# Three row buffers instead of four, and value tiles multiplied by column quarters, in the expert stage of a decoder step

## The chip, the cores and the metric

The kernel runs on one core of a Trainium2 chip. The metric is the time on the device in microseconds, the median of several runs.

## The reference

One layer of a decoder is applied to 256 prompt tokens and 8 x 8 sample tokens (320 rows of 2048): an attention with compressed, selected and window keys beside a short convolution, then an expert stage, then a gated embedding. The change lies in the expert stage. Each token picks, for each of 8 heads, 16 of 16384 experts; an expert is one row of `u_tab` and one row of `v_tab`, 2048 numbers each:

```python
def peer_ffn(n, wq, sub_keys, u_tab, v_tab):        # n: (320, 2048), normed
    ...
        g = jax.nn.softmax(fv, axis=-1)             # fv, eidx: the 16 best of each head
        act = jax.nn.gelu(jnp.einsum("td,trkd->trk", xc, u_tab[eidx]).astype(jnp.float32))
        return jnp.einsum("trk,trkd->td", (g * act).astype(xc.dtype), v_tab[eidx])
```

So every token reads 128 rows of `u_tab` (key rows) and 128 of `v_tab` (value rows), 8 KB each: 671 MB in all. The result is added to the residual `h`.

## The kernel before

Five engines run programs of their own and meet at semaphores. After the projections and the first attention work (about 750 us), the expert stage begins and goes on to about 2590 us. It is cut into 10 tiles `i` of 32 tokens, and each tile into 8 steps (`SSTEP`), 80 steps `k` in all (`STEPS`). On the 128 partitions of a step's tile lie 32 tokens four times over, and a step handles four rows `j` for each partition: four key tiles and four value tiles of 128 x 2048 floats.

A step passes through the engines like this:
- POOL (L586 to L601) issues four gathers of key rows into `u_row[0..3]` (L595), then four of value rows into `v_row[0..3]` (L600). Before it reuses a buffer it waits on `u_used` for key rows and on `v_used` for value rows. It works strictly in this order, and at a tile's first step it first waits for the indices (`idx_ready`).
- DVE (`group`, L1324) multiplies each key tile with the tokens' rows `n_rep` and sums along the row (L1333, one pass a tile, which gives `u_used`), waits for the GELU of ACT (`gelu`, L882), weighs the four results and builds `diag`, four 128x32 matrices that carry the weights (L1342, once a step).
- PE (`weighted_rows`, L1810) multiplies the value tiles with `diag` (L1821), in pairs `j = 0, 1` and `j = 2, 3`. Tile `j` writes column group `j` (partitions 32j to 32j+31) of four banks, one for each quarter `q` of the 2048 columns, so four partial sums of a quarter lie above each other. `v_used` goes up by 2 after each pair.
- At a tile's end ACT copies the banks to `acc` (`acc_out`, L886), PE adds the four groups with `sel` (L1830, 4 matmuls, `red_mm`), and DVE adds the result to `h` (`add_peer`, L1353, `h_seen`). PE starts the next tile's values only after `h_seen`. `acc_out` works in the same `acc` of which the first 32 partitions serve to stage the token rows of tiles 1 to 3 (`stage_rows`, L848, `spread_staged`).

Other work stands between the steps: in steps 0 to 31 (`EARLY`) PE runs `item(k)` (L1776) ahead of `weighted_rows(k)`, that is the rest of the attention, the projection with `w_out` (L1752, L1756) and the queries with `peer_wq` (L1772), with weights that SP loads. On DVE, pieces of `pick` (L1268) choose the next tile's experts between the steps. In steps 64 to 79 PE runs the gate matmuls (L1876) of the prompt after `weighted_rows(k)`. After step 79 come the gate of the sample rows and the outputs.

## Time and profile before

| what | value |
|---|---|
| median of 3 runs | 2659.68 us (2645.7 to 2661.2) |
| the profiled execution | 2654.51 us, of which the span of the page is 2652.7 us |
| granted TensorE clock, mean of the span | 0.823 |
| busy share of the span | PE 71%, PEld 34%, DVE 43%, ACT 13%, POOL 37% |
| DMA over the span | 871.89 MB, mean 329 GB/s, of it 671.13 MB by POOL's gathers |
| chain that ended last, by engine | PE 52%, DMA 34%, POOL 4%, DVE 4%, ACT 2% |

The page says how long each engine was busy, in which slices, which queue moved how much, and which chain of work ended last. The views of the trace show the same by stretches and single instructions. "Idle before" is the time in which the engine stood ahead of an instruction, and the arrow names what ended it.

### The profile page before, as it was taken

The numbers are of one execution on the slowest core, as the hardware profiler recorded it, in microseconds if no ns is written. First come the engines' busy times: TensorE is split into PE (matmuls) and PEld (weight loads), VectorE is DVE, ScalarE is ACT, GpSimd is POOL, SyncE is SP. The second block draws the span as 40 slices with busy tenths as digits, with TensorE's granted clock in tenths as the row PEclk, the third lists the DMA queues.
The fourth block names the chain that finished last, engine by engine and source line by source line (L and its number), as shares of the span: only waits on it lengthen the run. The fifth ranks groups of instructions, "written<-read, shape, count | busy, mean of one in ns | idle before, by whom it ended". The sixth has DMA issues, their size and how long they took to land.

```text
span 2652.7 us, 20815 instructions
## 1 busy us (share of the span) xinstructions
PE 1878.3 (71%) x8059; PEld 910.2 (34%) x8059; DVE 1153.9 (43%) x2082; ACT 335.1 (13%) x672; POOL 972.5 (37%) x644
## 2 busy tenths in 40 slices
PE   7999999989936668778789644444544534578788
PEld 3444445763912236423257311111111111222224
DVE  1000042231066753654452466566565675644442
ACT  1000002230012322110010110101001012000002
POOL 0000000000045643542352356666566665645540
PEclk9999998969967776689889776776767777799889
DMA  7463234526569998999899999999999999999996
GB/s 252 122 203 127 97 120 136 180 96 239 174 278 414 421 400 319 347 413 379 344 416 385 376 418 421 421 421 421 421 421 422 419 422 417 388 416 415 417 419 231
DMA packets 207430, 871.89 MB, mean 329 GB/s; under 512 B 24935, under 2 KB 49383, under 8 KB 123530
## 3 DMA queue, kind: packets, MB, share of 16 engines
q0 software_dynamic: 92160, 671.13, 61.4%
q1 hardware_dynamic: 115034, 198.74, 21.8%
q8 instruction: 58, 0.95, 0.1%
q10 hardware_dynamic: 144, 0.79, 0.1%
q14 instruction: 34, 0.28, 0.0%
HBM read 858.59 MB, written 12.95 MB: 329 GB/s over the span
## 4 chain that ended last, share of the span: by engine, by line
PE 52%; DMA 34%; POOL 4%; issue 4%; DVE 4%; ACT 2%; SPq 0%; DVEq 0%; PEldq 0%; ACTq 0%; POOLq 0%
DMA arena<-in_peer_v,arena 23%; PE bank L1821 15%; PE bank L1462 12%; DMA arena<-in_peer_u,arena 3%; POOL arena L600 3%; PE bank L1467 3%; DMA arena<-in_w_out 2%; PE bank L1512 2%; PE bank L1640 2%; DMA arena<-in_peer_wq 2%; PE bank L1616 2%; PE bank L1772 2%; PE bank L1876 2%; DMA arena<-in_state_win 2%; PE bank L1752 1%
## 5 line engine op out<-in xcount | busy, mean ns | idle before, releaser
L1821 PE MATMUL bank<-arena 128*32 128x512 f32 x2560 | 644.6, 714 | 614.9 <-DMA arena<-in_peer_v,arena 538.6
L1333 DVE CUSTOM_DVE_ANT_0 arena<-arena 128x2048 f32<-128x2048 f32 x320 | 732.1, 2292 | 641.3 <-DMA arena<-in_peer_u,arena 637.9
L600 POOL DMA_INDIRECT arena<-in_peer_v,arena x320 | 516.5, 1614 | 737.9 <-PE bank L1821 677.0
L595 POOL DMA_INDIRECT arena<-in_peer_u,arena x320 | 455.8, 1424 | 867.2 <-DVEq L1312 759.6
L1821 PEld LDWEIGHTS bank<-arena 128*32 128x32 f32 x2560 | 169.9, 129 | 1066.9 <-issue 993.7
L1462 PE MATMUL bank<-arena 128*128 128x512 f32 (+2 forms) x800 | 326.3, 567 | 7.0 <-PE bank L1467 5.7
L1462 PEld LDWEIGHTS bank<-arena 128*128 128x128 f32 (+1 forms) x800 | 147.4, 198 | 176.6 <-issue 176.5
L884 ACT ACTIVATE arena<-arena 128x4 f32<-128x4 f32 x80 | 16.4, 205 | 916.0 <-DVE arena L1333 915.8
L1876 PE MATMUL bank<-arena 128*128 128x512 f32 x256 | 112.7, 596 | 0.0
L1005 DVE TENSOR_TENSOR arena<-arena 128x1024 f32<-128x1024 f32 (+1 forms) x3 | 3.5, 1218 | 211.7 <-ACT arena L636 211.7
L1772 PE MATMUL bank<-arena 128*128 128x192 f32 x512 | 88.9, 337 | 9.3 <-DMA arena<-in_peer_wq 9.3
L1772 PEld LDWEIGHTS bank<-arena 128*128 128x128 f32 x512 | 87.2, 197 | 13.2 <-DMA arena<-in_peer_wq 9.9
L1752 PE MATMUL bank<-arena 128*128 128x512 f32 x128 | 68.1, 681 | 20.6 <-DMA arena<-in_w_out 20.6
L1467 PE MATMUL bank<-arena 128*64 128x256 f32 x704 | 80.8, 382 | 0.0
L1876 PEld LDWEIGHTS bank<-arena 128*128 128x128 f32 x256 | 48.0, 190 | 64.1 <-issue 64.1
L1020 DVE TENSOR_TENSOR arena<-arena 128x1024 f32<-128x1024 f32 (+1 forms) x21 | 24.4, 1218 | 102.0 <-DMA arena<-in_state_conv 101.8
L1436 PE MATMUL bank<-arena 128*128 128x128 f32 (+2 forms) x206 | 51.3, 356 | 21.5 <-issue 9.1
L1512 PE MATMUL bank<-arena 128*128 128x285 f32 x256 | 63.7, 412 | 1.3 <-ACT arena L661 0.7
L1467 PEld LDWEIGHTS bank<-arena 128*64 128x64 f32 x704 | 48.6, 137 | 39.0 <-issue 16.7
L1251 DVE MAX8 arena<-arena 128x8 f32<-128x128 f32 (+1 forms) x120 | 32.5, 326 | 66.3 <-ACT arena L755 63.8
L1830 PE MATMUL bank<-arena 128*32 128x512 f32 x80 | 44.7, 712 | 23.1 <-ACT arena L895 23.1
L1640 PE MATMUL bank<-arena 128*128 128x128 f32 x512 | 60.0, 281 | 1.2 <-PE bank L1640 0.6
(201 smaller groups left out, 1550.1 us busy)
## 6 DMA issues: line engine op xcount, KB each, us to landing
arena<-in_w_in SPq DMA_DIRECT2D x22, 2048.0 KB, 7.9
arena<-in_w_out SPq DMA_DIRECT2D x8, 2048.0 KB, 8.7
arena<-in_peer_wq SPq DMA_DIRECT2D x8, 2048.0 KB, 8.1
arena<-in_w_out SPq DMA_DIRECT2D x16, 1024.0 KB
arena<-in_peer_wq SPq DMA_DIRECT2D x16, 1024.0 KB
arena<-in_ple_gate SPq DMA_DIRECT2D x32, 512.0 KB, 16.3
arena<-in_ple_gate SPq DMA_DIRECT2D x6, 2048.0 KB, 11.6
arena<-in_cache_kv SPq DMA_DIRECT2D x64, 128.0 KB, 2.5
```

What stands on the lines that cost most here:

```text
L595: pool.indirect_dma_start(u_row[j], None, I["peer_u"][0], bass.IndirectOffsetOnAxis(idx[:, i, c + j:c + j + 1], 0)).then_inc(u_in[j], 16)
L600: pool.indirect_dma_start(v_row[j], None, I["peer_v"][0], bass.IndirectOffsetOnAxis(idx[:, i, c + j:c + j + 1], 0)).then_inc(v_in[j], 16)
L1333: dve.tensor_tensor_reduce(out=u_row[j], in0=u_row[j], in1=rep_of(i), scale=1.0, scalar=0.0, op0=ALU.mult, op1=ALU.add, accum_out=a4[:, pa ...
L1462: ins = pe.matmul(bank[3 * par + t][0:ROWS[t], 0:width], xT[:, 8 * half + k, 128 * t:128 * t + ROWS[t]], ring[slot][:, k, 0:width], start= ...
L1467: ins = pe.matmul(bank[3 * par + 2][64 * side:64 * side + 64, 0:256], xT[:, 8 * half + k, 256:TOK], ring[slot][:, k, 256 * side:256 * side ...
L1512: ins = pe.matmul(bank[hb][:, 0:(SEQS + 1) * NWIN], w1[:, m, hb * 128:hb * 128 + 128], view, start=(m == 0), stop=(m == BLK - 1))
L1616: ins = pe.matmul(bank[blk][:, :], xT_a[:, 8 * half + k, :], ring[slot][:, k, :], start=(half == 0 and k == 0), stop=(half == 1 and k == 7))
L1640: ins = pe.matmul(bank[4 * (n % 2) + sub][:, 0:128], ring[slot][:, k, 128 * sub:128 * sub + 128], nT_a[:, 8 * half + k, :], start=(half == ...
L1752: pe.matmul(bank[4 + 2 * (blk % 2)][:, :], xT_b[:, 4 * q + k, 0:128], ring_b[ring_of(f)][:, k, :], start=(q == 0 and k == 0), stop=(q == 3 ...
L1772: ins = pe.matmul(bank[4 + sub][:, 0:192], ring_b[ring_of(f)][:, k, 128 * sub:128 * sub + 128], nT_b[:, 4 * q + k, :], start=(q == 0 and k ...
L1821: ins = pe.matmul(bank[q][32 * j:32 * j + 32, :], diag[:, k % 2, j, :], v_row[j][:, 512 * q:512 * q + 512], start=(s == 0), stop=(s == SST ...
L1876: ins = pe.matmul(bank[4 + t][:, :], hT[:, 2 * part + k, 128 * t:128 * t + 128], gate_w[gate_slot(q)][:, k, :], start=(part == 0 and k == ...
```

## The change

It takes three buffers each for key rows and value rows (`RING = 3`), used in turn across steps by the number `n = 4k + j` of the tile; POOL waits, before gather `n`, for the use of tile `n - 3` of its kind. The value tiles get a matmul group each: tile `n` alone, its four column quarters `q` in the four column groups of one bank, and `v_used` goes up by 1 after each. All four tiles of a step and all steps of a tile of tokens add up in the same place of `bank[i % 2]`, so the sum over the column groups, its semaphores and its `sel` matmuls go. ACT copies the four groups of the bank into the tile's 32 rows of `acc`, DVE adds them to `h` in one instruction. The staged token rows lie in `acc[96:128]`. The order of the gathers, the order of PE's, ACT's and DVE's programs around them, and all other loads are as before.

```diff
+RING = 3
+    staged = acc[96:128, :]
-    u_row = [buf(W0 + j * D, D) for j in range(4)]
-    v_row = [buf(W0 + (4 + j) * D, D) for j in range(4)]
+    u_row = [buf(W0 + j * D, D) for j in range(RING)]
+    v_row = [buf(W0 + (4 + j) * D, D) for j in range(RING)]
...
             for j in range(4):
-                if k:
-                    pool.wait_ge(u_used, 4 * (k - 1) + j + 1)
-                pool.indirect_dma_start(u_row[j], None, I["peer_u"][0],
-                                        bass.IndirectOffsetOnAxis(idx[:, i, c + j:c + j + 1], 0)).then_inc(u_in[j], 16)
+                n = 4 * k + j
+                if n >= RING:
+                    pool.wait_ge(u_used, n - RING + 1)
+                pool.indirect_dma_start(u_row[n % RING], None, I["peer_u"][0],
+                                        bass.IndirectOffsetOnAxis(idx[:, i, c + j:c + j + 1], 0)).then_inc(u_in[n % RING], 16)
             for j in range(4):
-                if k:
-                    pool.wait_ge(v_used, 4 * (k - 1) + 2 * (j // 2) + 2)
-                pool.indirect_dma_start(v_row[j], None, I["peer_v"][0],
-                                        bass.IndirectOffsetOnAxis(idx[:, i, c + j:c + j + 1], 0)).then_inc(v_in[j], 16)
+                n = 4 * k + j
+                if n >= RING:
+                    pool.wait_ge(v_used, n - RING + 1)
+                pool.indirect_dma_start(v_row[n % RING], None, I["peer_v"][0],
+                                        bass.IndirectOffsetOnAxis(idx[:, i, c + j:c + j + 1], 0)).then_inc(v_in[n % RING], 16)
...
         def stage_rows(i):
             if i >= 2:
-                act.wait_ge(red_mm, i - 1)
-            act.dma_start(acc[0:32, :], n_dram[32 * i:32 * i + 32, :]).then_inc(stage_in, 16)
+                act.wait_ge(rep_act, i - 1)
+                act.wait_ge(rep_dve, i - 1)
+            act.dma_start(staged, n_dram[32 * i:32 * i + 32, :]).then_inc(stage_in, 16)
...
         def acc_out(i):
-            act.wait_ge(peer_mm, i + 1)
+            act.wait_ge(v_used, 4 * SSTEP * (i + 1))
             if i:
-                act.wait_ge(red_mm, i)
-            if i < 3:
-                act.wait_ge(rep_act, i + 1)
-                act.wait_ge(rep_dve, i + 1)
+                act.wait_ge(h_seen, i)
+            if i == 3:
+                act.wait_ge(rep_act, 3)
+                act.wait_ge(rep_dve, 3)
+            r = tile_of(i)[1]
             for q in range(4):
-                ins = act.activation(acc[:, 512 * q:512 * q + 512], bank[q][:, :], ACT.Copy)
+                ins = act.activation(acc[r:r + 32, 512 * q:512 * q + 512], bank[i % 2][32 * q:32 * q + 32, :], ACT.Copy)
             ins.then_inc(acc_ev, 1)
...
             for j in range(4):
-                dve.wait_ge(u_in[j], (k + 1) * 16)
-                dve.tensor_tensor_reduce(out=u_row[j], in0=u_row[j], in1=rep_of(i), scale=1.0, scalar=0.0,
+                n = 4 * k + j
+                dve.wait_ge(u_in[n % RING], 16 * (n // RING + 1))
+                dve.tensor_tensor_reduce(out=u_row[n % RING], in0=u_row[n % RING], in1=rep_of(i), scale=1.0, scalar=0.0,
                                          op0=ALU.mult, op1=ALU.add, accum_out=a4[:, par, j:j + 1]).then_inc(u_used, 1)
...
         def add_peer(i):
             t, r = tile_of(i)
-            dve.wait_ge(red_mm, i + 1)
-            for q in range(4):
-                v = h[r:r + 32, t, 512 * q:512 * q + 512]
-                ins = dve.tensor_tensor(v, bank[q][r:r + 32, :], v, ALU.add)
-            step(ins)
+            dve.wait_ge(acc_ev, i + 1)
+            v = h[r:r + 32, t, :]
+            step(dve.tensor_tensor(v, acc[r:r + 32, :], v, ALU.add))
             dve.sem_inc(h_seen, 1)
...
         def weighted_rows(k):
             i, s = divmod(k, SSTEP)
-            if s == 0 and i:
-                pe.wait_ge(h_seen, i)
+            if s == 0 and i >= 2:
+                pe.wait_ge(acc_ev, i - 1)
             pe.wait_ge(diag_ready, k + 1)
-            for j0 in (0, 2):
-                for j in (j0, j0 + 1):
-                    pe.wait_ge(v_in[j], 16 * (k + 1))
+            for j in range(4):
+                n = 4 * k + j
+                pe.wait_ge(v_in[n % RING], 16 * (n // RING + 1))
                 for q in range(4):
-                    for j in (j0, j0 + 1):
-                        ins = pe.matmul(bank[q][32 * j:32 * j + 32, :], diag[:, k % 2, j, :], v_row[j][:, 512 * q:512 * q + 512],
-                                        start=(s == 0), stop=(s == SSTEP - 1))
-                ins.then_inc(v_used, 2)
-            if s == SSTEP - 1:
-                pe.wait_ge(v_used, 4 * k + 4)
-                pe.sem_inc(peer_mm, 1)
-                pe.wait_ge(acc_ev, i + 1)
-                r = tile_of(i)[1]
-                for q in range(4):
-                    ins = pe.matmul(bank[q][r:r + 32, :], sel, acc[:, 512 * q:512 * q + 512], start=True, stop=True)
-                ins.then_inc(red_mm, 1)
+                    ins = pe.matmul(bank[i % 2][32 * q:32 * q + 32, :], diag[:, k % 2, j, :], v_row[n % RING][:, 512 * q:512 * q + 512],
+                                    start=(s == 0 and j == 0), stop=(s == SSTEP - 1 and j == 3))
+                ins.then_inc(v_used, 1)
```

## Rows read from the trace of the kernel before

**Rows 1.** The page: the span, and the chain that ended last by line.
```profile
span 2652.7 us, 20815 instructions
...
DMA arena<-in_peer_v,arena 23%; PE bank L1821 15%; PE bank L1462 12%; DMA arena<-in_peer_u,arena 3%; POOL arena L600 3%; PE bank L1467 3%; DMA arena<-in_w_out 2%; PE bank L1512 2%; PE bank L1640 2%; DMA arena<-in_peer_wq 2%; PE bank L1616 2%; PE bank L1772 2%; PE bank L1876 2%; DMA arena<-in_state_win 2%; PE bank L1752 1%
```

**Rows 2.** By stretches, L1342 alone: length, busy (count), PE clock, DMA share, GB/s.
```profile
760.00:940.00 180.00, 2.63 (x9) 0.76 1.01 419
940.00:1500.00 560.00, 5.54 (x19) 0.81 0.95 373
1500.00:2212.00 712.00, 10.49 (x36) 0.71 1.01 420
2212.00:2600.00 388.00, 4.67 (x16) 0.86 1.00 409
```

**Rows 3.** The page's costliest groups: busy, mean ns, then idle before and its end.
```profile
L1821 PE MATMUL bank<-arena 128*32 128x512 f32 x2560 | 644.6, 714 | 614.9 <-DMA arena<-in_peer_v,arena 538.6
...
L600 POOL DMA_INDIRECT arena<-in_peer_v,arena x320 | 516.5, 1614 | 737.9 <-PE bank L1821 677.0
```

**Rows 4.** Timeline 1620 to 1660: start, length, engine, line, operation, idle before.
```profile
1625.73 2.62 POOL L595 DMA_INDIRECT arena<-in_peer_u,arena  x1 [0.30 <-issue]
...
1640.28 2.29 DVE L1333 CUSTOM_DVE_ANT_0 arena<-arena 128x2048 f32<-128x2048 f32 x1 [7.34 <-DMA arena<-in_peer_u,arena]
...
1640.37 3.02 POOL L600 DMA_INDIRECT arena<-in_peer_v,arena  x1 [0.30 <-issue]
...
1642.66 2.29 DVE L1333 CUSTOM_DVE_ANT_0 arena<-arena 128x2048 f32<-128x2048 f32 x1
...
1647.64 2.29 DVE L1333 CUSTOM_DVE_ANT_0 arena<-arena 128x2048 f32<-128x2048 f32 x1 [0.19 <-DMA arena<-in_peer_u,arena]
...
1650.48 0.29 DVE L1342 TENSOR_TENSOR arena<-arena 128x128 f32<-128x128 f32 x1
```

**Rows 5.** Timeline, the first gather of all and the first pass on it.
```profile
752.25 1.08 POOL L595 DMA_INDIRECT arena<-in_peer_u,arena  x1 [751.79 <-DVEq L1312]
...
758.29 2.29 DVE L1333 CUSTOM_DVE_ANT_0 arena<-arena 128x2048 f32<-128x2048 f32 x1 [6.25 <-DMA arena<-in_peer_u,arena]
```

**Rows 6.** Timeline, a second value gather of a step and PE's start on it.
```profile
2294.32 2.15 POOL L600 DMA_INDIRECT arena<-in_peer_v,arena  x1 [0.31 <-issue]
...
2301.57 8.95 PE L1821 MATMUL bank<-arena 128*32 128x512 f32 x32 [6.01 <-DMA arena<-in_peer_v,arena]
```

**Rows 7.** Timeline, a key gather that waited for a DVE pass.
```profile
2227.89 2.29 DVE L1333 CUSTOM_DVE_ANT_0 arena<-arena 128x2048 f32<-128x2048 f32 x1
...
2230.11 2.29 DVE L1333 CUSTOM_DVE_ANT_0 arena<-arena 128x2048 f32<-128x2048 f32 x1
2230.46 2.75 POOL L595 DMA_INDIRECT arena<-in_peer_u,arena  x1 [4.53 <-DVE arena L1333]
```

**Rows 8.** Timeline, value matmuls: weight loads at 1.2 and 2.4 GHz, one half step.
```profile
1653.56 0.21 PEld L1821 LDWEIGHTS bank<-arena 128*32 128x32 f32 x2 [0.64 <-issue]
...
1654.41 0.21 PEld L1821 LDWEIGHTS bank<-arena 128*32 128x32 f32 x2 [0.64 <-issue]
...
2423.39 3.63 PE L1821 MATMUL bank<-arena 128*32 128x512 f32 x16 [1.92 <-DMA arena<-in_peer_v,arena]
...
1233.33 0.15 PEld L1821 LDWEIGHTS bank<-arena 128*32 128x32 f32 x4 [0.28 <-issue]
...
1233.76 0.15 PEld L1821 LDWEIGHTS bank<-arena 128*32 128x32 f32 x4 [0.28 <-issue]
```

**Rows 9.** The chain in order of time, in a step with `w_out`.
```profile
1207.36 15.86 DMA arena<-in_w_out
...
1231.23 5.31 PE bank L1821 x32
```

**Rows 10.** The chain in order of time, after the last step.
```profile
2596.87 5.29 PE bank L1830 x8
```

**Rows 11.** Timeline, POOL's wait for the indices of tile 4.
```profile
1573.62 0.94 POOL L595 DMA_INDIRECT arena<-in_peer_u,arena  x1 [7.82 <-DVEq L1312]
```

More of the change, by code:

```diff
@@ L225, in build @@
     u_used, v_used = sem("u_used"), sem("v_used")
-    u_in = [sem(f"u_in{j}") for j in range(4)]
-    v_in = [sem(f"v_in{j}") for j in range(4)]
+    u_in = [sem(f"u_in{j}") for j in range(RING)]
+    v_in = [sem(f"v_in{j}") for j in range(RING)]
     n_out = sem("n_out")
@@ L230, in build @@
     src_in = [None, sem("src_in1"), sem("src_in2")]
-    gelu_done, weighed, diag_ready, peer_mm, acc_ev, red_mm = map(sem, (
-        "gelu_done", "weighed", "diag_ready", "peer_mm", "acc_ev", "red_mm"))
+    gelu_done, weighed, diag_ready, acc_ev = map(sem, ("gelu_done", "weighed", "diag_ready", "acc_ev"))
     ple_in, ple_used = [sem("ple_in0"), sem("ple_in1")], sem("ple_used")
@@ L857, in spread_staged @@
             for g in range(2):
-                ins = act.activation(n_rep[0][32 * g:32 * g + 32, :], acc[0:32, :], ACT.Copy)
+                ins = act.activation(n_rep[0][32 * g:32 * g + 32, :], staged, ACT.Copy)
             ins.then_inc(rep_act, 1)
@@ L1348, in spread_staged @@
             for g in (2, 3):
-                ins = dve.tensor_copy(n_rep[0][32 * g:32 * g + 32, :], acc[0:32, :])
+                ins = dve.tensor_copy(n_rep[0][32 * g:32 * g + 32, :], staged)
             step(ins)
```

1 line of the change is left out of this document (removed).

## The prediction

> **What bounds the kernel now.** I read the page first: its span and the chain that ended last. The largest part of that chain is the gathers of value rows, then the matmuls on them (L1821) [rows 1]. The view by stretches, cut to the 80 instructions that build `diag` (L1342, one a step), gives the pace [rows 2]: 9 steps in 760 to 940 (20.0 us each), 19 in 940 to 1500 (29.5), 36 in 1500 to 2212 (19.8), 16 in 2212 to 2600 (24.3). Beside them stands the DMA: 419 to 420 GB/s at a full share in the first and third stretch, 373 at 0.95 in the second, 409 in the last. A step gathers 8 tiles of 128 x 2048 x 4 bytes, 1.05 MB each; at 420 GB/s a tile is 2.49 us and eight are 19.9 us. So 45 steps run at the pace of the DMA engines alone, and every engine waits for them: over the run PE's value matmuls stood 539 us for value rows, and POOL 677 us for buffers that PE gives back [rows 3]. There the kernel is bound by transfers as long as enough of them are queued.
>
> How many are queued decides this change. The gather of a step's first key tile ended its issue at 1628.35 and the DVE pass on it began at 1640.28: 11.9 us in the queue [rows 4]. The shortest way from the end of an issue to the landing is seen with empty queues: issue done at 753.33, DVE starts at 758.29, so 4.8 to 5.0 us [rows 5]; issue done at 2296.47, PE starts on that tile at 2301.57, 5.1 us less the wake-up [rows 6]. I use 4.8, of which 2.49 is moving.
>
> **What the change does to the gathers.** POOL issues in order: four keys, four values. With four buffers each, the keys of the next step never wait for themselves. With three, the fourth key tile (call it u3) waits until the DVE pass on u0 of the same step is done, and v3 until PE has used v0 of the same step, and nothing of the next step can be issued ahead of v3. Two loops through landing latency arise in each step. Take u0's landing as 0.
> 1. DVE starts at 0.12 and passes follow at about 2.38 to 2.49 while the data comes at 2.49 [rows 4], so on u1 at 2.61. POOL starts 2.57 after the start of the pass that frees its buffer (2227.89 to 2230.46) [rows 7], so at 2.69, when the next pass is on. An issue caught by a pass ends 0.81 after that pass: the pass from 1640.28 to 1642.57 held POOL to 1643.39 [rows 4]; the pass 2230.11 to 2232.40 held it to 2233.21 [rows 7]. Hence u3's issue ends at 2.61 + 2.29 + 0.82 = 5.7 and u3 lands at 10.5, not at 7.47: 3.0 us lost.
> 2. v0's issue starts at 6.0, is caught by the pass on u2 and ends at 8.2; it lands behind u3 at 13.0, v1 at 15.5, v2 at 18.0. `diag` is ready 3.13 after the last pass begins (1647.64 to 1650.77 [rows 4]): 10.6 + 3.1 = 13.8.
> 3. PE on v0. A 128x512 matmul is two records (2560 for 80 steps of 16) [rows 3]. At the slow clock pairs of loads come each 0.85 us, at the fast each 0.43 [rows 8]. A half step of 16 records, on two column groups, takes 3.63 at the fast clock [rows 8]: two at a time. Where both halves overlap, four loads come each 0.43 us [rows 8], so four groups do run side by side. Then a value tile is two passes: 1.7 us slow, 0.9 fast. PE will have idled long before each tile and the bursts get short, so I take slow: v0 is done at 15.7. (Two at a time: 17.4. Fast: 14.9.)
> 4. POOL wakes 0.3 later (as after the pass that ended at 2230.18 [rows 7]), ends the issue of v3 at 16.9, v3 lands at 21.7 (without a gap: 20.5), the next u0 at 24.2.
>
> The step becomes 24.2 instead of 19.9, +4.3 us. For the 45 steps at the DMA's pace: +194 us.
>
> By the Trainium skill, "DMA: Bandwidth & Descriptors", section "Anatomy of one DMA", a gather costs about 2.0 us plus its bytes at 436 GB/s, 4.4 us for this size. The trace has 4.8 to 5.0, and goes first. By the page's figure each loop would be 0.4 shorter, the step 23.4, and the sum some 36 us less.
>
> **940 to 1500 (19 steps).** PE's other work sets the pace here: in the chain such a step is a wait of 15.9 us for the last of the weights, their matmuls, and the value burst of 5.3 [rows 9]. Up to now all values lie ready when PE comes to them. After, only three do: PE uses v0 (0.9), POOL issues v3 (0.3 + 0.94), 4.8 to land, 0.9 to 1.7 to multiply, 8 to 8.6 us in place of 5.3, about +3. The following gathers then start later too, with less loaded in advance, but the weights fill the engines meanwhile. I take +3.5, from 0 (the wait falls in a wait for weights) to +8 (it adds to it, and PE's clock sinks in the new gaps): 19 x 3.5 = +66.
>
> **2212 to 2600 (16 steps).** The gate weights run beside the gathers. The 4.3 us a step in which the gathers leave the DMA idle can carry them, so the step is not 24.3 + 4.3. Nor is it less than 24.2, and a block of gate matmuls can lie in front of v0's use. I take 26.5: +2.2 each, +35 (0 to +70).
>
> **Ends of tiles.** The sum over the four column groups goes: eight records of L1830, the wait of PE for `acc`, the `h_seen` wait before the next burst. Inside the gather stretches this lies under the DMA queue (the share stays full through all ends in 1500 to 2212 [rows 2]) and gives nothing. At the very end it is on the path: L1830's 5.3 us [rows 10], and four adds from PSUM against one from SBUF of the same elements: -7. The new waits of ACT and PE (on `h_seen`, on `acc_ev` of the tile before last) are met a whole tile earlier: nothing. POOL's wait for the indices of tile 4, 7.8 us before 1573.62, lay under the tiles still queued [rows 11]; now it comes behind v3 with three buffers loaded: +5, once. The first three tiles' staging in `acc[96:128]` moves no load: nothing, while the copy on DVE and ACT ends within a step.
>
> **Sum.** 2652.7 + 194 + 66 + 35 - 7 + 5 = 2945.7. The profiled execution took 2654.5 against a median of 2659.7 and a lowest of 2645.7, so a median might be 5 more; rounded down for the clock of PE, which may be fast at some tiles: 2940.
>
> **Rivals.**
> - *POOL is not caught by the passes.* If POOL's start falls just ahead of the pass on u1 (they are 0.08 apart in step 1), u3's issue ends at 3.6, u3 lands at 8.4, and the same walk gives u0 at 22.0: +2.1 a step, 45 x 2.1 = 95. With 50 for the second stretch and 20 for the third and -2: 2816; with the fast clock 2755. For it: 0.08 is small. Against: data that comes at 2.49 or sooner starts the next pass 2.38 to 2.49 after the one before [rows 4], and POOL needs 2.57 [rows 7].
> - *The column groups don't run four wide on different quarters of one tile.* Then v0 is done at 17.4 and a step is 25.9: 45 x 6.0 = 270, 19 x 6 = 114, 16 x 4 = 64, -2: 3099. For it: the half steps ran two wide [rows 8]. Against: that is the two groups they use, and the four loads per 0.43 us. The Trainium skill, "TensorEngine Tiling (Array Packing)", section "Overview", has up to 4x for a stationary of 32 columns; the overlap of the halves is the only row that bears on it.
> - *The transfers stay hidden, no change.* The queue held 11.9 us and needs 4.8; 7.1 us spare is more than two buffers (5.0 us) [rows 4, 5]. Then the DMA stays full and only the end gains: 2646. Against: the count looks at the average depth, while u3 waits behind a landing with two tiles (5.0 us) left to come and needs 2.6 + 0.94 + 4.8 - 2.49.
> - *Faster.* PE's savings in 940 to 1500 decide, with the gathers full: the burst falls from 5.3 [rows 9] to 8 passes of 0.43, 3.4: 19 x -1.9 = -36, three sums over groups -16, the end -7: 2594. It decides only if an issue lands within 3.8 us (7.47 - 2.69 - 0.94); both rows of an empty queue have 4.8 or more [rows 5, 6].
>
> **How the numbers follow.** Forecast 0.57, POOL not caught 0.19, not four wide 0.13, hidden 0.06, faster 0.05. Around 1% is what a measurement of this kernel can tell from no change. Faster by over 1%: 0.05; within 1%: 0.06; slower: 0.89. The forecast's own range is 2830 to 3020 (second stretch 0 to +152, third 0 to +70, PE's clock -0.8 a step). The range for 8 in 10 takes in the first rival down to its fast-clock end, 2755, and goes up to 3050, into the second rival's lower part.
>
> **What would show it.** In 1500 to 2212: 24 us between `diag` builds in place of 19.8, DMA at 347 GB/s in place of 420, POOL's largest wait on L1333 or before the fourth key issue, with that issue lasting over 2 us, DVE waiting some 5 us before the fourth pass and not for the three before; PE at half its clock (1.2 GHz) and tiles of 1.7 us; PE waiting on v3 in 940 to 1500. I am wrong if the DMA stays at 420 there (hidden), if the fourth key issue takes 0.94 (not caught), or if a tile's eight records take over 3 us (not four wide).

## The result, and the profile after

| kernel | median us | runs | us, lowest to highest | profiled span us |
|---|---|---|---|---|
| before | 2659.93 | 4 | 2645.7 to 2661.2 | 2652.7 |
| changed | 3012.63 | 4 | 3008.78 to 3017.6 | 3015.8 |

The changed kernel is slower by 13.4%: the ratio is 1.1343, with a 95% interval of 1.1315 to 1.1371. The forecast of 2940 was 73 us too low. 3012.63 lies inside the range of 2755 to 3050, and inside the forecast's own range of 2830 to 3020 by 7 us.

The page of the changed kernel: span, the chain that ended last by line, and the groups of value matmuls and of the two kinds of gather (count, busy us, mean ns, idle before and what ended it). They answer to [rows 1, 3].

```profile
span 3015.8 us, 20527 instructions
...
DMA arena<-in_peer_u,arena 30%; PE bank L1466 11%; DVE arena L1339 9%; DMA arena<-in_peer_v,arena 6%; PE bank L1822 5%; POOL arena L603 3%; PE bank L1471 3%; PE bank L1516 2%; PE bank L1776 2%; DMA arena<-in_w_out 2%; PE bank L1644 2%; PE bank L1620 2%; PE bank L1869 2%; PE bank L1756 2%; POOL arena L597 1%
...
L1822 PE MATMUL bank<-arena 128*32 128x512 f32 x2560 | 545.0, 951 | 1108.9 <-DVE arena L1348 732.8
...
L597 POOL DMA_INDIRECT arena<-in_peer_u,arena x320 | 434.9, 1359 | 1451.6 <-DVEq L1317 756.4
L603 POOL DMA_INDIRECT arena<-in_peer_v,arena x320 | 430.6, 1345 | 628.2 <-PE bank L1822 548.5
```

Before, the chain ran through value rows (23%) and the matmuls on them (15%). Now key rows hold 30% of it, the DVE pass 9%, and PE's value matmuls 5%: ahead of these PE stands 733 us for the `diag`. A share of 30% for key rows does not mean that only they are late; the chain passes through their landing because the loop closes there.

By stretches, each cut at a `diag` build of the same step as in [rows 2] (L1348 now): length, busy and count, PE clock, DMA share, GB/s.

```profile
766.00:974.00 208.00, 2.62 (x9) 0.62 0.88 339
974.00:1622.00 648.00, 5.54 (x19) 0.73 0.87 334
1622.00:2500.00 878.00, 10.49 (x36) 0.53 0.87 336
2500.00:2944.00 444.00, 4.66 (x16) 0.73 0.89 345
2944.00:3015.00 71.00, 0.00 (x0) 0.80 0.66 242
```

The DMA moves 339, 334, 336 and 345 GB/s in the four stretches of the expert stage, where it moved 419, 373, 420 and 409. PE's granted clock is 0.53 in the third stretch: it ran at its lower level, 1.2 GHz, nearly all the time.

For the account by steps, count the 80 `diag` builds from 0. Their starts in the timelines:

| | diag 0 | 8 | 28 | 63 | 79 | span |
|---|---|---|---|---|---|---|
| before | 769.04 | 934.55 | 1508.66 | 2211.50 | 2582.65 | 2652.7 |
| changed | 775.17 | 973.64 | 1623.13 | 2497.04 | 2943.05 | 3015.8 |
| added | +6.1 | +33.0 | +75.4 | +171.1 | +74.9 | +2.7 |

The sum is 363.1, the difference of the spans (the entries are rounded). The 43 steps that were at the DMA's pace (0 to 8, 28 to 63) cost 204 us, 4.75 each; from 28 to 63 a step is 24.97 us in place of 20.08.

One such step in the timeline of the changed kernel (start, length, engine, line, operation, idle before):

```profile
1927.36 0.94 POOL L603 DMA_INDIRECT arena<-in_peer_v,arena  x1 [6.52 <-issue]
...
1928.60 0.94 POOL L597 DMA_INDIRECT arena<-in_peer_u,arena  x1 [0.30 <-issue]
...
1932.92 1.93 PE L1822 MATMUL bank<-arena 128*32 128x512 f32 x8 [2.06 <-DMA arena<-in_peer_v,arena]
1936.08 2.29 DVE L1339 CUSTOM_DVE_ANT_0 arena<-arena 128x2048 f32<-128x2048 f32 x1 [8.17 <-DMA arena<-in_peer_u,arena]
...
1938.46 2.29 DVE L1339 CUSTOM_DVE_ANT_0 arena<-arena 128x2048 f32<-128x2048 f32 x1
1938.65 2.92 POOL L597 DMA_INDIRECT arena<-in_peer_u,arena  x1 [6.63 <-DVE arena L1339]
...
1941.88 2.33 POOL L603 DMA_INDIRECT arena<-in_peer_v,arena  x1 [0.30 <-issue]
...
1946.18 2.29 DVE L1339 CUSTOM_DVE_ANT_0 arena<-arena 128x2048 f32<-128x2048 f32 x1 [2.78 <-DMA arena<-in_peer_u,arena]
...
1949.02 0.29 DVE L1348 TENSOR_TENSOR arena<-arena 128x128 f32<-128x128 f32 x1
...
1949.36 1.93 PE L1822 MATMUL bank<-arena 128*32 128x512 f32 x8 [14.51 <-DVE arena L1348]
...
1951.60 0.94 POOL L603 DMA_INDIRECT arena<-in_peer_v,arena  x1 [4.90 <-PE bank L1822]
...
1952.84 0.94 POOL L597 DMA_INDIRECT arena<-in_peer_u,arena  x1 [0.30 <-issue]
```

The reader is to follow two waits. POOL stood 6.63 us for the pass on u0, then its fourth key issue began 0.19 us into the next pass and took 2.92 us; u3 was used at 1946.18. And POOL stood 4.90 us for PE's matmuls on v0, which stood 14.51 us for the `diag`; only then v3 was asked for, and behind it u0 to u2 of the next step.

What the DMA does meanwhile, in slices of 2 us (length, busy and count of PE, weight loads, DVE, ACT and POOL, PE clock, DMA share, GB/s):

```profile
1928.00:1930.00 2.00, 1.43 (x12) 0.20 (x8) 0.00 (x0) 0.00 (x0) 1.39 (x3) 0.50 0.54 102
1930.00:1932.00 2.00, 0.86 (x5) 0.00 (x0) 0.00 (x0) 0.00 (x0) 1.70 (x2) 0.50 0.98 410
...
1940.00:1942.00 2.00, 0.00 (x0) 0.00 (x0) 1.66 (x3) 0.00 (x0) 1.70 (x2) 0.50 0.06 25
1942.00:1944.00 2.00, 0.00 (x0) 0.00 (x0) 1.40 (x2) 0.00 (x0) 2.00 (x1) 0.50 0.86 217
```

There are two holes in this step, one in front of v3's transfer (102 GB/s) and one in front of u3's (25, then 217 GB/s). In between the DMA is busy, but not at its old pace: the other slices of this step moved 356 to 426 GB/s. From the shares of the stretches an estimate can be made of the two parts. Now 0.87 of 24.97 us is 21.7 us of busy DMA a step; before, a full share of 20.08 us moved the same bytes. So about 3.2 us of the 4.9 a step are idle DMA, and about 1.6 us are transfers that take longer while the DMA is busy.

### The profile page after: what moved, and what is told of

Its sections match the earlier page's. It is cut to its first block, busy times and chain, and to the rows that moved or that the text cites. A ratio compares the mean times of both kernels' runs of the same rounds, so it can differ in the third digit from the quotient of the medians.

```text
span 3015.8 us, 20527 instructions
## 1 busy us (share of the span) xinstructions
PE 1777.2 (59%) x7979; PEld 821.7 (27%) x7979; DVE 1150.9 (38%) x2052; ACT 338.5 (11%) x672; POOL 865.6 (29%) x644
## 4 chain that ended last, share of the span: by engine, by line
DMA 38%; PE 37%; DVE 12%; issue 6%; POOL 5%; ACT 2%; SPq 0%; DVEq 0%; PEldq 0%; ACTq 0%; POOLq 0%
DMA arena<-in_peer_u,arena 30%; PE bank L1466 11%; DVE arena L1339 9%; DMA arena<-in_peer_v,arena 6%; PE bank L1822 5%; POOL arena L603 3%; PE bank L1471 3%; PE bank L1516 2%; PE bank L1776 2%; DMA arena<-in_w_out 2%; PE bank L1644 2%; PE bank L1620 2%; PE bank L1869 2%; PE bank L1756 2%; POOL arena L597 1%
## 5 line engine op out<-in xcount | busy, mean ns | idle before, releaser
L1822 PE MATMUL bank<-arena 128*32 128x512 f32 x2560 | 545.0, 951 | 1108.9 <-DVE arena L1348 732.8
L597 POOL DMA_INDIRECT arena<-in_peer_u,arena x320 | 434.9, 1359 | 1451.6 <-DVEq L1317 756.4
L603 POOL DMA_INDIRECT arena<-in_peer_v,arena x320 | 430.6, 1345 | 628.2 <-PE bank L1822 548.5
L1822 PEld LDWEIGHTS bank<-arena 128*32 128x32 f32 x2560 | 66.8, 134 | 1536.0 <-DVE arena L1348 769.6
L1869 PE MATMUL bank<-arena 128*128 128x512 f32 x256 | 123.2, 640 | 0.0
L1776 PEld LDWEIGHTS bank<-arena 128*128 128x128 f32 x512 | 86.9, 197 | 6.7 <-issue 6.7
L1756 PE MATMUL bank<-arena 128*128 128x512 f32 x128 | 75.4, 744 | 16.9 <-DMA arena<-in_w_out 16.9
L1869 PEld LDWEIGHTS bank<-arena 128*128 128x128 f32 x256 | 52.2, 208 | 75.4 <-issue 75.4
L1644 PEld LDWEIGHTS bank<-arena 128*128 128x128 f32 x512 | 59.4, 197 | 1.9 <-issue 1.2
L1620 PE MATMUL bank<-arena 128*128 128x512 f32 x128 | 57.4, 607 | 1.0 <-DVE arena L1191 0.5
```

The costliest lines, as they stand in the source:

```text
L597: pool.indirect_dma_start(u_row[n % RING], None, I["peer_u"][0], bass.IndirectOffsetOnAxis(idx[:, i, c + j:c + j + 1], 0)).then_inc(u_in[n ...
L603: pool.indirect_dma_start(v_row[n % RING], None, I["peer_v"][0], bass.IndirectOffsetOnAxis(idx[:, i, c + j:c + j + 1], 0)).then_inc(v_in[n ...
L1620: ins = pe.matmul(bank[blk][:, :], xT_a[:, 8 * half + k, :], ring[slot][:, k, :], start=(half == 0 and k == 0), stop=(half == 1 and k == 7))
L1644: ins = pe.matmul(bank[4 * (n % 2) + sub][:, 0:128], ring[slot][:, k, 128 * sub:128 * sub + 128], nT_a[:, 8 * half + k, :], start=(half == ...
L1756: pe.matmul(bank[4 + 2 * (blk % 2)][:, :], xT_b[:, 4 * q + k, 0:128], ring_b[ring_of(f)][:, k, :], start=(q == 0 and k == 0), stop=(q == 3 ...
L1776: ins = pe.matmul(bank[4 + sub][:, 0:192], ring_b[ring_of(f)][:, k, 128 * sub:128 * sub + 128], nT_b[:, 4 * q + k, :], start=(q == 0 and k ...
```

## The experiments

The runs form five questions. Periods are us from `diag` to `diag`; the plain stretch is from 28 to 63. GB/s is that of 1650 to 2200.

| kernel | time us | 0 to 8 | 8 to 28 | 28 to 63 | 63 to 79 | GB/s |
|---|---|---|---|---|---|---|
| before | 2659.9 | 20.69 | 28.71 | 20.08 | 23.20 | 421 |
| changed | 3012.6 | 24.81 | 32.47 | 24.97 | 27.88 | 336 |
| r44 | 2655.5 | 20.31 | 28.68 | 20.09 | 23.12 | 422 |
| r43 | 2815.3 | 21.90 | 31.16 | 21.90 | 25.05 | 384 |
| r34 | 2877.9 | 24.01 | 29.46 | 23.73 | 26.16 | 354 |
| yield33 | 2949.5 | 24.10 | 30.90 | 24.74 | 26.82 | 339 |
| wait33 | 2904.3 | 23.35 | 31.21 | 23.49 | 26.45 | 357 |
| late33 | 2851.9 | 22.66 | 31.02 | 22.33 | 26.08 | 379 |
| late_wait33 | 2809.8 | 23.12 | 31.24 | 21.27 | 24.98 | 394 |
| pairq33 | 3244.0 | 27.90 | 33.18 | 28.69 | 31.14 | 292 |
| pairs33 | 3401.6 | 30.45 | 35.59 | 30.88 | 32.19 | 273 |
| gate33 | 2982.7 | 24.57 | 31.36 | 24.86 | 27.52 | 338 |
| r33 | 3021.8 | 24.68 | 32.54 | 24.77 | 28.09 | 339 |
| lategate44 | 2665.5 | 21.40 | 28.26 | 20.09 | 23.28 | 421 |

r44, r33 and lategate44 are medians of 4 to 10 runs; the others below the changed kernel are one execution each.

### Which part of the change costs: r44, r43, r34

The kernels are the changed one with the number of buffers given for keys and values apart (4 and 4, 4 and 3, 3 and 4):

```diff
-RING = 3
+RU, RV = 4, 4
...
-                if n >= RING:
-                    pool.wait_ge(u_used, n - RING + 1)
+                if n >= RU:
+                    pool.wait_ge(u_used, n - RU + 1)
```

and the same with `RV` at the value gathers, DVE's and PE's waits and the buffers.

> The changed kernel with four buffers of each kind again; matmuls, sums and release of single value tiles as in the change. Loop theory (the two waits with three buffers are all of the loss): the gathers are full again, DMA about 420 GB/s and 19.9 us a step in the plain stretch, and the whole is before's time less the last sum over the column groups and what the shorter bursts give in the stretch of the projections: 2635, from 2610 to 2660. Matmul theory (column quarters and single tiles themselves cost): stays above 2750.

Measured: 2655.48, ratio to before 1.0011 (0.9992 to 1.0029). The column quarters, the single release and the sums that are gone move nothing while the DMA is full. The stretch 1650 to 2200 of r44 (columns as in the slices above):

```profile
1650.00:2200.00 550.00, 172.57 (x888) 20.65 (x880) 336.16 (x558) 52.35 (x66) 334.46 (x220) 0.63 1.01 422
```

PE is busy 172.57 us of 550 there; in the same stretch of before it is 254.8. A third less busy time on PE, and the same step. The expected gain was not there either in 8 to 28, where I had looked for it: 28.68 against 28.71.

> Four key buffers, three value buffers. Loop theory: the wait of the fourth key gather on the first DVE pass is gone (3.0 us a step), the wait of the fourth value gather on PE stays: u3 lands at 7.5, diag 10.7, v0 used 12.7, v3 traffic starts 1.3 late, and restarts cost some: 21.9 us a step in the plain stretch, about 2790 in all, and the DVE waits before the passes are even. Buffer-count theory (only the number of tiles that can be under way counts, 7 of 8 in either mix): the same as with three keys and four values, about 2830.

> Three key buffers, four value buffers. Loop theory: the wait of the fourth key gather stays whole, caught by the next DVE pass, so 3.0 us and a restart, 23.2 us a step in the plain stretch, about 2835 in all, longer than with four keys and three values by some 45. Buffer-count theory: the same as that kernel.

Measured: 2815.3 and 2877.9, 25 and 43 us above what was expected, in the expected order. Both have seven buffers and differ by 63 us, so the theory that only their number counts is out. In the plain stretch the loss of the fourth value buffer alone costs 1.82 us a step (21.90 - 20.08), that of the fourth key buffer alone 3.65, both 4.89. So all of the slowdown is in the ring sizes, and the two loops overlap by 0.6 us. In 63 to 79 it is +1.85 and +2.96 against the kernel before, both together +4.68, and r44 has -0.08.

In 8 to 28 it is the other way round: values +2.45 a step, keys +0.75. These are single executions, and the kernels with three and three buffers and single value tiles spread from 30.9 to 32.5 there, so +0.75 is not clear of that spread. What grows in this part is the wait in front of the value matmuls, as their group shows for `diag` 10 to 22, before and changed (busy us, mean ns, idle before):

```profile
L1821 PE MATMUL bank<-arena 128*32 128x512 f32 x384 | 81.2, 682 | 35.6 <-DMA arena<-in_peer_v,arena 26.5 <-DVEq L1360 5.5 <-DVE arena L1342 3.7
```

```profile
L1822 PE MATMUL bank<-arena 128*32 128x512 f32 x384 | 69.6, 841 | 99.0 <-DMA arena<-in_peer_v,arena 66.0 <-DVE arena L1348 33.0
```

That part is 55.4 us longer (356.5 to 411.9), and this wait 63.4 us.

### Is the caught issue worth its microseconds: yield33, wait33

yield33 lets DVE wait before its second pass for an increment that stands behind the fourth key gather in POOL's program:

```diff
+                if j == 3:
+                    pool.sem_inc(u3_out, 1)
...
+                if j == 1:
+                    dve.wait_ge(u3_out, k + 1)
```

> The changed kernel (three and three), but DVE waits ahead of its pass on a step's second key tile until POOL has issued the fourth key gather; nothing else. Loop theory with the catch: that issue takes 0.94 instead of 3.0, u3 lands 2 us earlier, DVE loses 1.2 us a step that lie under the wait for u3; the first value issues are then caught instead. 22.6 us a step in the plain stretch in place of 24.9, about 2890 in all. If the catch were no cost of its own (the landing latency is all), DVE's stop only adds: 24.9 or more, 3010 or more.

Measured: 2949.5, and 24.74 us in the plain stretch. The edit did not do what it was for, as its timeline shows:

```profile
1914.03 2.29 DVE L1344 CUSTOM_DVE_ANT_0 arena<-arena 128x2048 f32<-128x2048 f32 x1 [0.20 <-POOLq L601]
1914.11 3.03 POOL L598 DMA_INDIRECT arena<-in_peer_u,arena  x1 [6.96 <-DVE arena L1344]
```

DVE was released by POOL's queue 0.08 us before the gather's own record begins, and the issue was caught all the same (3.03 us). So the increment does not say that the issue is over. This run decides nothing on the catch; it is 63 us faster than the changed kernel mostly outside the plain stretch (see the last question).

wait33 puts a write on POOL itself between, and DVE waits for that:

```diff
+    mark = buf(W0 + 3 * D, 1)
...
+                if j == 3:
+                    pool.memset(mark, 0.0).then_inc(u3_out, 1)
```

> The changed kernel, where POOL writes one column of 128 words behind the issue of the fourth key gather and DVE waits for that write before the pass on the second key tile, so that the issue is over when the pass begins (the increment from POOL's queue in yield33 came as soon as the issue had begun, and its pass began 0.08 us before the issue's record: the issue was caught there as well, 3.03 us). Theory: being caught costs about 2 us a step, since the fourth key tile and every transfer behind it start 2 us later: the issue takes some 0.9 us instead of 2.9, the pass on u1 begins about 1.3 us later, 23.0 us a step in place of 25.0 where steps are plain, and with what yield33 gained elsewhere 2860 us in all (2830-2920). Rival: the catch is hidden behind the three value tiles, and only DVE is late by 1.3 us: 25 us a step or more, 2950 us or above.

Measured: 2904.3. The timeline:

```profile
1903.80 2.29 DVE L1345 CUSTOM_DVE_ANT_0 arena<-arena 128x2048 f32<-128x2048 f32 x1 [10.01 <-DMA arena<-in_peer_u,arena]
...
1906.37 0.94 POOL L599 DMA_INDIRECT arena<-in_peer_u,arena  x1 [7.57 <-DVE arena L1345]
1907.30 0.12 POOL L602 MEMSET arena<- 128x1 f32 x1
1907.46 2.29 DVE L1345 CUSTOM_DVE_ANT_0 arena<-arena 128x2048 f32<-128x2048 f32 x1 [1.36 <-POOL arena L602]
1907.61 2.95 POOL L607 DMA_INDIRECT arena<-in_peer_v,arena  x1 [0.19 <-issue]
```

The key issue takes 0.94, DVE's second pass starts 1.36 late, and now the next issue, v0's, is caught (2.95). The step falls from 24.97 to 23.49: 1.48 us of the 1.97 expected. Against yield33, whose DVE waits as well but whose issue is caught, it is 1.25. So the catch is on the path, and 1.3 to 1.5 of its two microseconds were worth having.

### Is it the order of the queue or the number of buffers: late33, late_wait33

late33 gathers v3 of a step behind u0 to u2 of the next:

```diff
...
+            for j in range(3):
+                key_gather(4 * k + j)
+            if k:
+                value_gather(4 * k - 1)
+            key_gather(4 * k + 3)
+            for j in range(3):
+                value_gather(4 * k + j)
...
```

> Three buffers a side and the single value tiles as in the changed kernel; alone the order of the gathers differs: the fourth value tile of a step is gathered after the first three key tiles of the next step, where in the changed kernel those three stand behind it on POOL's queue. The theory of the loop (u0 of the next step cannot be asked for before the fourth value tile, which waits for the matmuls on the first, which wait for the diag) says that this order breaks it: from a diag it takes 2.3 us for the pass on u0, some 7.5 for the fourth key tile to be issued and land, 2.3 and 3.4 to the next diag, in all some 16 us, under the 20.1 us that eight tiles take at full rate, so 20.4 to 21.5 us a step from diag to diag in the stretch 1500-2212 of before and 2700 us in all (2670-2760). The rival, that six buffers instead of eight leave too little in flight in whatever order, says 24 us a step or more and over 2930 us.

Measured: 2851.9 and 22.33 us: between the two theories. Moving one gather gives back 2.64 of the 4.89 us; the prediction's loop over v3 was real. But the step does not reach 20.4 to 21.5. Its timeline shows what is left of the two loops:

```profile
1905.02 0.94 POOL L598 DMA_INDIRECT arena<-in_peer_v,arena  x1 [0.30 <-issue]
...
1912.42 2.90 POOL L591 DMA_INDIRECT arena<-in_peer_u,arena  x1 [6.47 <-DVE arena L1347]
...
1917.20 1.94 PE L1830 MATMUL bank<-arena 128*32 128x512 f32 x8 [8.03 <-DMA arena<-in_peer_v,arena]
...
1919.44 0.94 POOL L598 DMA_INDIRECT arena<-in_peer_v,arena  x1 [0.39 <-PE bank L1830]
```

v3 now lands behind three key tiles, and is used 11.2 us after its issue ended (1905.96 to 1917.20). v2 of the next step needs that buffer, and u0 to u2 stand behind it on POOL's queue, but in this step v2 waited only 0.39 us. Over 28 to 63 POOL stood 57.9 us for PE's value matmuls, where it stood 171.4 in the changed kernel, and 261.6 us for DVE's passes, where it stood 245.9: the order shortens the loop over v3 and leaves the one over u3, with its caught issue (2.90 us at 1912.42).

late_wait33 has the edits of late33 and wait33.

> Both edits at once: the fourth value gather behind the next step's first three key gathers (late33, 22.33 us a step) and DVE waiting until the fourth key gather is issued (wait33, 23.49 against 24.97). In the trace of late33 the third value gather waited for the matmuls on the fourth tile of the step before, which landed 12 us after its issue behind three key tiles; the catch of the key issue lies in front of that wait and is mostly covered by it. Theory: what remains is then set by six buffers: 22.0 us a step (21.4-22.5), 2830 us (2800-2860). Rival: the two gains add, 20.9 us a step and 2760 us or less.

Measured: 2809.8 and 21.27 us, again between: waiting for the issue gives another 1.06 us on top of the order, of the 1.48 that it gave alone. The DMA in 1650 to 2200:

```profile
1650.00:2200.00 550.00, 193.66 (x826) 21.76 (x822) 309.76 (x491) 46.78 (x65) 317.41 (x235) 0.53 0.99 394
```

A share of 0.99 moves 394 GB/s here, where 1.01 moved 421. So of 4.89 us a step, 3.70 go back with six buffers and the two edits. The last 1.2 us were not taken apart; at a share of 0.99 they are hardly idle DMA, but transfers that take longer. The time of 2809.8 lies in the theory's range, its step under it.

### What the single release and the quarters are worth with three buffers: pairs33, pairq33

pairs33 is the kernel before with three buffers a side and nothing else of the change:

```diff
...
+                n = 4 * k + j
+                if n >= 3:
+                    m = n - 3
+                    pool.wait_ge(v_used, 4 * (m // 4) + 2 * (m % 4 // 2) + 2)
...
```

> The kernel before with its pairwise matmuls (two column groups at a time, sums in four banks, and the addition over row groups at the end of a tile) and its release of value buffers two at a time, with three buffers a side: the first part of the change alone. The fourth value gather then waits for both of the first two value tiles, multiplied together in 3.63 us at half clock [half a step of before], in place of one tile in 1.93: the loop is 1.7 us longer, up to 2.5 where the second tile is late. Expected 26.7 to 27.5 us a step in the plain stretch against 25.0 of after, and 3170 us in all (3110-3230). Rival: the single release and the column quarters are worth nothing since transfers alone set the step: 25.0 us a step and 3020 us.

Measured: 3401.6 and 30.88 us a step, far above. The expectation rests on a misread row: the half step of 3.63 us is at the fast clock, as the prediction has it, not at half clock. The timeline of pairs33:

```profile
1911.12 6.58 PE L1825 MATMUL bank<-arena 128*32 128x512 f32 x16 [9.26 <-DMA arena<-in_peer_v,arena]
...
1917.97 0.94 POOL L603 DMA_INDIRECT arena<-in_peer_v,arena  x1 [9.05 <-PE bank L1825]
```

A pair takes 6.58 us at 1.2 GHz, and POOL's fourth value gather starts 0.27 us after it has ended.

pairq33 is the changed kernel with buffers waited for and released in pairs; POOL's wait for value buffers is that of pairs33:

```diff
...
-                pe.wait_ge(v_in[n % RV], 16 * (n // RV + 1))
+                if j % 2 == 0:
+                    pe.wait_ge(v_in[n % RV], 16 * (n // RV + 1))
+                    pe.wait_ge(v_in[(n + 1) % RV], 16 * ((n + 1) // RV + 1))
...
-                ins.then_inc(v_used, 1)
+                if j % 2:
+                    ins.then_inc(v_used, 2)
```

> The changed kernel with its four column groups, but value buffers waited for and released two at a time, as before: it stands between pairs33 (30.9 us a step) and after (25.0) and splits their 5.9 us. Theory: in pairs33 the pair took 6.58 us at half clock, two groups wide; here two tiles take 3.87, so the fourth value gather waits 1.9 us longer than in after: 26.9 us a step in the plain stretch, 3165 us in all (3110-3210), which gives 4 us of the 5.9 to the width and 1.9 to the release. Rival: the release is what matters, since the second tile lands late, and 29 us a step or more, over 3300 us.

Measured: 3244.0 and 28.69 us. The chain in order of time:

```profile
1915.36 7.46 DMA arena<-in_peer_v,arena
...
1922.96 3.67 PE bank L1825 x16
```

v1 is what PE waits for: the `diag` of that step began at 1920.24, and in the changed kernel PE begins on v0 0.34 us after that (1949.02 to 1949.36), so it could have begun at 1920.6, 2.4 us before the pair. Then two tiles take 3.67 in place of one in 1.93. That makes 4.1 us in this step; 3.72 a step were measured. Both theories had a part of it. So the single release is worth 3.7 us a step and the four groups 2.2 (30.88 - 28.69), where I had expected 1.9 and 4. The kernel that only cut the buffers would have lost twice what this change lost.

### The last stretch, and a better kernel: gate33, r33, lategate44

gate33 moves the gate's sigmoid behind the gelu and the prompt's output behind the `diag`:

```diff
-            if i in (6, 9, 12):
-                gate_sigmoid((i - 6) // 3)
             gelu(k)
+            if i in (6, 9, 12):
+                gate_sigmoid((i - 6) // 3)
...
+            if k - LAST in behind:
+                behind[k - LAST]()
```

> The changed kernel, with two pieces of the gate moved behind the expert step they stand in, four times in all: the sigmoid behind the gelu on ACT, and the prompt's output behind the diag on DVE. Theory: in the steps of 31 to 34 us in the stretch 2500-2944 of after, the diag waited for a gate block on PE that itself began only when the last value tile had landed; with the move the diag waits for neither, those four steps fall to about 26 us, the stretch from the 64th to the 80th diag goes from 27.9 us a step to about 26.3, and the whole to 2988 us (2975-3000). Rival: these steps are long because PE has the gate block to do anyway before it can free value buffers, so the stretch stays at 27.5 to 28 and the time at 3013 us.

The expectation says four times; there are three such places, steps 70, 73 and 76. In the changed kernel, step 73:

```profile
2762.19 1.94 PE L1822 MATMUL bank<-arena 128*32 128x512 f32 x8 [1.52 <-DMA arena<-in_peer_v,arena]
...
2764.06 14.64 PE L1869 MATMUL bank<-arena 128*128 128x512 f32 x32
...
2778.82 1.26 ACT L883 ACTIVATE arena<-bank,arena 128x512 f32<-128x512 f32 x2 [26.03 <-PEq L1874]
...
2781.44 1.29 DVE L1380 TENSOR_TENSOR arena<-arena 128x512 f32<-128x512 f32 x2
...
2783.15 0.29 DVE L1348 TENSOR_TENSOR arena<-arena 128x128 f32<-128x128 f32 x1
```

The last pass ended at 2776.03, and the `diag` came 7.1 us later, not 0.6, since it stood behind the sigmoid and L1380. With the move the three steps fall from 32.3, 31.4 and 31.7 us to 27.2, 27.5 and 27.6, a little over the 26 expected. But most of the steps behind them grow (24.6 to 26.8, 26.6 to 27.3, 23.5 to 26.5; one goes from 27.7 to 27.3), and over 63 to 79 only 5.8 us are left, 27.52 a step. The rival is nearly right: what is not waited for in one step is for the most part waited for in the next.

gate33 is all the same 30 us faster, which puts its time into the theory's range by luck: 22 of the 30 us lie in 8 to 28, where nothing was edited. yield33 and wait33 have the like there.

r33 is the changed kernel with `RU, RV = 3, 3` in place of `RING = 3`.

> A control: the changed kernel as it is, only with the one constant for the number of buffers written as two constants that are both 3. gate33, wait33 and yield33 all ran the stretch from the 8th to the 28th diag 22 to 31 us shorter than the changed kernel (31.4, 31.2 and 30.9 us a step against 32.5), where their edits do nothing that I can name. Theory: that belongs to the execution, not to the edits, and this kernel shows where it falls: 3013 us (2980-3020), 31.0 to 32.6 us a step there, and 25.0 in the plain stretch. Rival: the edits did it, and this kernel repeats 32.5 us a step there and 3010 to 3018 us.

Measured: 3021.8 (3013.4 to 3025.7, ratio 1.138, 1.1358 to 1.1403) and 32.54 us a step in 8 to 28: the changed kernel repeats itself there, as the rival says. The time itself is a little above both ranges. One thing that differs shows in the groups of that part, `diag` 10 to 22, first of the changed kernel, then of gate33 (busy us, mean ns, idle before):

```profile
L1756 PE MATMUL bank<-arena 128*128 128x512 f32 x128 | 75.4, 744 | 16.9 <-DMA arena<-in_w_out 16.9
```

```profile
L1758 PE MATMUL bank<-arena 128*128 128x512 f32 x128 | 62.2, 630 | 3.8 <-DMA arena<-in_w_out 3.8
```

The matmuls with `w_out` wait 13.1 us less for their weights and run 13.2 us shorter, 26 us together. In r33 the same group has 9.7 us of waiting and 71.5 busy, 11 us less than the changed kernel, and its step is no shorter, so this group is not the whole of it. Why the weights come earlier with an edit that touches only steps from 70 on is open. r33 and gate33 ran on different chips. The kernel before took 2655.9 us on the chip of r33 and 2663.8 beside gate33, so the chips do not differ the way that the two kernels do, but with so few runs a part of the chip is not excluded.

lategate44 has the edits of r44, late33 and gate33 together.

> Four buffers a side with the column quarters (r44: 2655.5 us, as before), the fourth value gather behind the next step's first three key gathers, and the gate's sigmoid and prompt output behind the expert step they stand in. Theory: with four buffers the transfers fill the plain stretch (1.01 of the time at 422 GB/s in r44, 20.1 us a step) and nearly fill the last one (before: 409 GB/s), so neither edit has anything to give back: 2650 us (2635-2662), not distinguishable from before at 1%. Rival: in the stretch from the 8th to the 28th diag (28.7 us a step, 0.95 of the time) and in the last one the steps of 31 to 45 us come from waits of this order, and the time falls to 2620 us or less.

Measured: 2665.5, ratio 1.0042 (1.0019 to 1.0065): the theory's answer, but 3.5 us above its range and 0.4% slower than before. With four buffers the transfers set the pace and no order gives anything. No version here beats the kernel before.

## Why the prediction was right in kind and 73 us low

1. *The fourth key gather waits for u0's pass and is caught by the next.* Right. With u0 landed at 1935.96 as zero (0.12 before the pass, as in the prediction), the issue ended at 5.6 (5.7 predicted) and u3 was used at 10.2 (10.6). The reason of the rival "not caught" was weighed rightly: POOL started 2.57 after the pass, DVE 2.38. wait33 shows that the catch costs 1.3 to 1.5 us a step.
2. *`diag`, v0 and v3.* Right to 0.5 us: `diag` ready at 13.35 (13.8), v0 done at 15.3 (15.7), v3's issue done at 16.6 (16.9). Tiles of 1.93 us at 1.2 GHz, four groups wide (1.7 predicted). The wait for v3 as a loop is shown by late33: 2.64 us.
3. *The landing, and the step.* Mis-sized. From the end of an issue to the landing with little queued it was 4.5 us (1928.30 to 1932.8, 1941.57 to 1946.06), not 4.8. By the Trainium skill, "DMA: Bandwidth & Descriptors", section "Anatomy of one DMA", it would be 4.4, an estimate from a fixed 2.0 us and the bytes at 436 GB/s, and the trace all but agrees; but the step did not come out shorter for it. (Of the prediction's two rows for an empty queue the second is none: the gather ahead of it had ended its issue at 2294.02 and was still under way.) The median of 27 plain steps has v3 landing at 21.9, 5.3 after its issue ended, near the 21.7 of the prediction: an issue that ends 0.3 sooner and a landing that takes 0.5 longer make up for each other, which is luck. From there the next u0 took 3.1 us, not 2.49, and the step became 24.97, not 24.2. So the term that was too small is the time of a tile behind a hole; why it takes longer is open. The stretches from 0 to 8 and from 28 to 63 gave 204 us, the prediction had 194; they have 43 steps where it counted 45, so at 4.75 each its own count would give 214.
4. *940 to 1500.* +75.4 against +66. Near, and the reason holds: r43 shows that the value buffers cost most there (2.45 us a step), as the prediction says, and the wait in front of the value matmuls is what grew (35.6 to 99.0 us in `diag` 10 to 22). The `w_out` group has 88.7 us of waiting and work before and 92.3 after, so it hardly adds to this. That other kernels with three buffers a side are up to 1.6 us a step faster there is open, and makes the size of this term less sure than its cause.
5. *2212 to 2600.* The step that failed: +74.9 against +35, above its bound of 70. It has two faults. The first is the pace of before: 388 us for 16 steps is 24.3, but the window goes on 17 us behind the last `diag`, and from `diag` to `diag` it was 23.20. The forecast of 26.5 a step would have been +53 by that. The second is that the prediction took the idle DMA to be a place for the gate weights. But the DMA that stands in a latency loop did not give its idle time to this stretch: the loop's 4.7 us came on top (27.88 - 23.20 = 4.68), as in the plain stretch, and r44, r43 and r34 show that the ring sizes alone bring it (-0.08, +1.85 and +2.96). The gate block of PE stands in the loop as well, by 14.6 us at a time, and gate33 shows that moving what waits for it hardly helps.
6. *The ends.* -7 at the very end became +2.7. The chain after the last step of the changed kernel:

```profile
2944.77 9.27 DMA arena<-in_peer_v,arena
...
2954.08 1.98 PE bank L1822 x8
...
2958.49 1.28 ACT L883
...
2963.81 5.10 PE bank L1883 x8
```

 The sum over groups is gone, but the sigmoid and the output of the last gate block (5.2 us from 2958.49 to 2963.71) had been hidden beside L1830; they are on the path now. I had priced what went and not asked what it covered. r44 has the same chain and gains 1.3 us at the end, not 7. Most of the other 4.0 us is the late last v3: PE is done with it 13.0 us after the last `diag`, in r44 9.4. POOL's wait for the indices of tile 4, +5, did not come: no step from 30 to 36 is over 26.2 us. The first `diag` is 6.1 us late, but 4.7 of that lie ahead of the loops: the first gather began at 756.90, not at 752.25, since it waited longer for DVE's indices. It began at 754.44 in r33 and at 752.13 in yield33, so this is not the rings; why is open.

The terms of the forecast's sum against the measured ones: 10 us for the plain steps, 9 for the second stretch, 40 for the third, 10 for the end, 1 for the start and the indices; together 70, the distance of 2945.7 from 3015.8. The 1 is luck: the wait that was priced at 5 did not come, and a start 6 us late that nobody priced did. The rival "not four wide" is out: 1.93 us a tile at 1.2 GHz, 1.07 at 2.4. The Trainium skill, "TensorEngine Tiling (Array Packing)", section "Overview", says up to 4x for such a stationary; the traces show 1.7x from two groups to four (6.58 us for two tiles against 1.93 for one), and no run here has one group alone.

## What to carry to other kernels

Count buffers against the longest chain that the order of the issuing queue closes (landing, use, release, issue, landing), not against the mean depth of the queue: two buffers fewer of eight made a step 24% longer here, and moving one gather in the queue gave back over half. Release a buffer as soon as its own tile is used; with few buffers that was worth more than wider matmuls, and with enough buffers neither was worth anything. Idle DMA in a latency loop was not room for other transfers here, and work that is taken off the end uncovers what lay beside it.

## What the runs showed of the hardware

- A gather issued by POOL just after a DVE pass over 128 x 2048 has begun takes 2.9 to 3.0 us in place of 0.94; with the pass held back, the same issue takes 0.94 and the next one 2.95 (wait33). The catch moves rather than goes.
- A plain increment on POOL's queue behind a gather was seen by DVE 0.08 us before the gather's record began (yield33). A write on POOL itself behind it was seen after the issue ended, at 0.16 us after the start of the write (wait33).
- The share of busy DMA does not tell the rate: 1.01 moved 421 GB/s, 0.99 moved 394, 0.87 moved 336, which is 417, 398 and 386 for a full share. A hole costs more than its own length: the slice behind one had 217 GB/s at a share of 0.86 in 2 us.
- PE's clock fell to 1.2 GHz in the waits of the changed kernel (0.53 in the third stretch, 0.71 before), and a record of the value matmuls took a mean of 951 ns against 714. A value tile is 1.93 us in place of 1.07. Only v0's is in the loop, so by estimate the clock is worth up to 0.9 us of the 4.9 a step; no run tested it.
